# Expert stage of a hybrid decoder layer: from blocks of 64 rows on two column halves to steps of two 32-row sub-blocks on four column quarters

## The reference, cut to what matters

```
x1 = x + mix(rms_norm(x)) @ w_out            # attention, convolution and SSM heads
h  = rms_norm(x1)
group  = argmax(h @ group_w + group_b)        # 1 of 4 groups
expert = top 2 of the 8 experts of that group
y[t]   = sum over its 2 experts e: gate * ((silu(h@w_gate[e]) * (h@w_up[e])) @ w_down[e])
out    = rms_norm(x1 + y)
```

```
31 46 51 266 10 71 8 71 28 41 58 11 47 24 36 213 18 108 47 82 38 60 42 179 16 29 99 81 8 67 73 89
```

## Time and profile before

| what | value |
|---|---|
| median of 3 runs | 1182.27 us (1181.92 to 1182.78) |
| the profiled execution, its own time | 1182.57 us |
| its span | 1180.8 us |
| expert stage: first up/gate matmul to the end of the span | 565.6 to 1180.8 us |
| TensorE busy, share of the span | 94% |
| VectorE, ScalarE, GpSimd busy | 50%, 30%, 35% |

### The profile page before, as it was taken

One profiled execution on the slowest core, in us unless ns is written; L12 is line 12 of the kernel. 1 busy time (PEld: TensorE's weight loads), 2 busy tenths in 40 slices (PEclk: granted clock), 3 DMA queues, 4 the chain that ended last, 5 costly groups with the idle time before them and its releaser, 6 DMA issues.

```text
span 1180.8 us, 16952 instructions
## 1 busy us (share of the span) xinstructions
PE 1115.6 (94%) x5082; PEld 545.8 (46%) x5083; DVE 588.6 (50%) x1347; ACT 356.5 (30%) x719; POOL 410.9 (35%) x359
## 2 busy tenths in 40 slices
PE   5999999999999999997799999977999999999993
PEld 5898444445456666656333333322333333333331
DVE  3560009954556666546255554533454545555452
ACT  3222100025655555422132332312223323232231
POOL 0110099950000001010244545443345454444542
PEclk9999999999999999998899999989999999999998
DMA  8126212021231111159593799999969999999811
GB/s 265 25 37 126 53 22 52 8 71 39 96 157 62 58 43 54 55 226 369 191 403 80 286 391 392 413 407 415 413 248 406 407 417 413 402 416 402 349 29 33
DMA packets 91596, 257.71 MB, mean 218 GB/s; under 512 B 38867, under 2 KB 56026, under 8 KB 66942
## 3 DMA queue, kind: packets, MB, share of 16 engines
q1 hardware_dynamic: 66580, 234.78, 51.8%
q0 software_dynamic: 19232, 21.06, 6.5%
q10 hardware_dynamic: 5706, 0.92, 0.4%
HBM read 253.51 MB, written 35.13 MB: 244 GB/s over the span
## 4 chain that ended last, share of the span: by engine, by line
PE 83%; DMA 9%; ACT 2%; DVE 2%; issue 1%; SPq 1%; POOL 0%; ACTq 0%; DVEq 0%; POOLq 0%
PE psum L1386 25%; PE psum L1081 14%; PE psum L1405 12%; PE psum L1279 9%; DMA W<-in_w_down 5%; PE psum L1078 4%; PE psum L1224 3%; PE psum L1244 3%; DMA W<-in_w_gate 3%; PE psum L1076 3%; PE psum L1372 2%; PE psum L1235 2%; PE psum L1393 2%; PE psum L1308 1%; DMA W<-in_x 1%
## 5 line engine op out<-in xcount | busy, mean ns | idle before, releaser
L1386 PE MATMUL psum<-W,band 128*64 x400 | 187.7, 614 | 15.3 <-DVE W L1935 15.3
L1387 PE MATMUL psum<-W,band 128*64 128x512 f32 x400 | 187.7, 614 | 0.0
L1386 PE MATMUL psum<-W,RD 128*64 (+1 forms) x400 | 182.9, 601 | 2.5 <-DVE W L1935 1.5
L1405 PE MATMUL psum<-W,RD 128*64 (+1 forms) x400 | 180.0, 593 | 4.2 <-ACT RD L1010 2.6
L1387 PE MATMUL psum<-W,RD 128*64 128x512 f32 x400 | 182.9, 601 | 0.0
L1406 PE MATMUL psum<-RD 128*64 128x512 f32 x400 | 180.0, 593 | 0.0
L735 POOL DMA_INDIRECT x_rows<-RD,tabf x48 | 78.4, 1633 | 276.9 <-ACT RD L1018 266.0
L1081 PE MATMUL psum<-W 128*128 128x512 f32 x384 | 166.9, 594 | 0.4 <-ACT W L824 0.4
L1279 PE MATMUL psum<-W,RD 128*128 128x512 f32 x256 | 118.2, 594 | 1.6 <-ACT RD L900 1.1
L1081 PEld LDWEIGHTS psum<-W 128*128 128x128 f32 x384 | 72.5, 191 | 88.0 <-issue 87.1
L1386 PEld LDWEIGHTS psum<-W,band 128*64 128x64 f32 x400 | 54.0, 141 | 123.8 <-issue 120.8
(11 more groups left out here) (330 smaller groups left out, 1762.0 us busy)
## 6 DMA issues: line engine op xcount, KB each, us to landing
W<-in_w_up SPq DMA_DIRECT2D x32, 2048.0 KB, 13.2
W<-in_w_gate SPq DMA_DIRECT2D x32, 2048.0 KB, 19.0
W<-in_w_down SPq DMA_DIRECT2D x32, 2048.0 KB, 21.7
W<-in_x SPq DMA_DIRECT2D x16, 512.0 KB, 4.7
W<-in_w_in SPq DMA_DIRECT2D x5, 1024.0 KB, 11.6
W<-in_w_in SPq DMA_DIRECT2D x16, 256.0 KB, 4.4
x_rows<-W SPq DMA_DIRECT2D x8, 512.0 KB, 2.9
h_rows<-RD SPq DMA_DIRECT2D x8, 512.0 KB, 3.6
```

The lines of the kernel that those rows point to most:

```text
L1386: pe.matmul(bank(2)[0:HALF].rearrange("p (g n) -> p g n", g=2), x, near, start=k == 0, stop=k == KD - 1)
L1387: ins = pe.matmul(bank(2)[HALF:P], x, upgate1[:, k].rearrange("p g n -> p (g n)"), start=k == 0, stop=k == KD - 1)
L1405: pe.matmul(out[0:HALF], a, W[:, bass.ds(base + (2 * KD * FF + D * k), 512)], start=k == 0, stop=k == FK - 1)
```

## The change

Each expert now gets ceil(rows / 32) sub-blocks, at least one, 81 in all. A step takes two consecutive sub-blocks, A and B, each with its own expert, which may be the same: 41 steps. Each product over k is four matmuls on the four column quarters (32 rows held each): A near from the slot in place, A far from `farA`, B near and B far from `bothB`. ScalarE copies `farA` (512 numbers per partition and k), VectorE copies `bothB` (1024). Both are rings of four k steps, so a copy waits until the quarter products that used its buffer last are done (`used`), and the products of each k wait for both copies (`copied`). The square and sum of the finished rows moves from VectorE to ScalarE (`row_sum`). On GpSimd the rows come in earlier in the step, behind a wait for a scatter (`added`). All steps are written out, 32 of them always run, up to 16 more in nested conditions. `MAXPAIR` is 48. Lines that only rename or resize are left out below.

```diff
+def up_lap(b, part): return part if b == 0 else 3 * b - 1 + part
+def down_lap(b): return 3 * b + 4
...
+        def used(lap, j):        # the semaphore and value that tell that lap's use of buffer j is over
...
 pool.block_io(b):
-                if b >= 2:
-                    pool.wait_ge(ex_ye, b - 1)
-                    if b >= 3:
-                        pool.wait_ge(scat_out[(b - 1) % 2], 16 * ((b - 1) // 2))
-                    (scatter-add of block b-2)
+                if b >= 3:
+                    added(b - 3)
+                if b >= 1:
+                    x_in_rows(b - 1)
+                if b >= 2:
+                    pool.wait_ge(ex_ye, b - 1)
+                    (scatter-add of pair b-2)
                 gather(b + AHEAD); x_out_rows(b - 3); root(b - 2)
-                x_in_rows(b)
...
 act:
+            def step(b, before):
+                base, loads = tables(b)
+                silu_gate(b - 1)
+                weights_in(wug_in, loads, 32)
+                for j in range(4): far_up(base, up_lap(b, 0), j, j)
+                y_evac(b - 2)
+                for j in range(4): far_up(base, up_lap(b, 1), j, 4 + j)
+                actT_evac(b - 1)
+                row_sum(b - 2)
+                weights_in(wd_in, before[1], 16)
+                for k in range(FK): far_down(before[0], down_lap(b - 1), k)
...
 pe, for each k of up_gate (and alike for down):
-                    pe.matmul(bank(2)[0:HALF], x, near, ...)
-                    ins = pe.matmul(bank(2)[HALF:P], x, upgate1[:, k], ...)
+                    copied(lap, j)
+                    pe.matmul(out[0:SUB], xA, near, ...)
+                    pe.matmul(out[SUB:2 * SUB], xA, farA[j], ...)
+                    pe.matmul(out[2 * SUB:3 * SUB], xB, bothB[j][:, 0:512], ...)
+                    ins = pe.matmul(out[3 * SUB:P], xB, bothB[j][:, 512:1024], ...)
+                    ins.then_inc(ex_u if part == 1 and j == 3 else ex_k, 1)
+            def step(b, before):
+                up_gate(base, b, 0); aT(b - 1); xT(b + 1); up_gate(base, b, 1)
+                down(before, b - 1, down_lap(b - 1))
...
 dve:
+            def both_up(base, lap, j, k):
+                free(lap, j)                                  # wait for used(lap - 1, j)
+                dve.tensor_copy(bothB[j] ..., up and gate of k, all 2 x 512 columns).then_inc(ex_cB, 1)
+            def step(b, before):
+                base, loads = tables(b)
+                weights_in(wug_in, loads, 32)
+                both_up(0), both_up(1)
+                act_mul(b - 1)
+                both_up(2), both_up(3), both_up(4), both_up(5)
+                rows_add(b - 2)
+                both_up(6), both_up(7)
+                xT_evac(b + 1)                                # two instructions of 256 numbers
+                weights_in(wd_in, before[1], 16)
+                both_down(0), both_down(1)
+                rows_scale(b - 3)
+                both_down(2), both_down(3)
+                mean_square(b - 2)                            # four on 32 partitions each, one on 128
```

## The result

| | before | after |
|---|---|---|
| median of the comparison's runs | 1182.53 us (1181.92 to 1184.46, 4 runs) | 1204.93 us (1202.64 to 1207.33, 4 runs) |
| ratio, 95% interval | 1 | 1.0187 (1.016 to 1.0214) |
| the profiled execution, its span | 1182.57, 1180.8 us | 1206.59, 1204.5 us |
| TensorE, VectorE, ScalarE, GpSimd busy | 94, 50, 30, 35% | 86, 61, 47, 32% |
| mean granted clock of the span | 0.983 | 0.961 |

The change makes the kernel 1.9% slower, where 0.3% faster was forecast: 26 us off, inside the stated range. The step count (41) and the bounding engine are as forecast; the step is longer.

A forecast was written before the change was run, and what follows sets the result against it. VectorE was to bound the kernel at 13.3 us a step (TensorE 11.37). Expert 14's gate at 807.05 + 8.6 + 2.5 + 25 steps (332.5) + 0.6 + 2, then 24 to the end: span 1177.3, time 1179 us, range 1158 to 1222.

The forecast's parts named there:

- waits for the ring: VectorE's copies waiting for TensorE to free buffers: none expected, each free in time, slack 0.2 us in a 13.3 us step.
- GpSimd's hold: Rival: five GpSimd instructions each hold a VectorE copy 0.25 us; step 14.5, 1216 us; chance 0.21, shared with other waits.
- GpSimd gives way: GpSimd issues meeting VectorE copies: the issue stretches (2.29 us, median 1.05), copies keep their time; hidden under 13.3 us.
- the centre: The central forecast: VectorE's step 13.3 us, time 1179 us; chance 0.53 for a step of 13.0 to 13.7.
- The copies' sum: VectorE's step: 2.95 us to the first copy, twelve copies at 0.60 (7.2), plus smaller operations, 13.3 us.
- The clock: Rival: TensorE idles about 2 us every step, its clock falls each time, adding 2.5: step 15.8, 1256 us; chance 0.06.
- Late loads: Steps 10 to 16 wait some 40 us for weights; expert 14's gate lets VectorE copy at 807.05, no later waits.
- TensorE's overlap: Groups of four products run fully abreast, 0.853 us a group, step 11.37; rival of incomplete overlap, up to 1466 us, chance 0.06.
- ScalarE: ScalarE's step: twelve copies 6.5 us, other work about 2, reads and waits at most 2.95; 11.4, hidden under 13.3.

The follow-up runs named there:

- the new order: Changed kernel with VectorE's row scaling ahead of the first down copy and mean square ahead of the last: 1188.76 us; also without scatters and later gathers: 1163.93 us.

## Why the prediction was wrong

**The step that failed** is the account of what holds VectorE. It has two terms at nothing, waits for the ring and GpSimd's hold, and each alone makes the step 13.7 us: the first by the run without scatters and gathers, the second worked out from the trace of the changed kernel. The first is the account of waits: "With the first copy at 0, TensorE starts at 0.7 ... the first down copy at 6.5 needs the buffer used at 6.1. The slack is thin, 0.2 us, so 13.3 leans upward." Measured from the first copy: TensorE starts at 0.94 (911.62), not 0.7; its second group of part 1 starts at 6.31 (916.99), so the first buffer is used by then and the second by 7.17; VectorE starts the second down copy at 7.53, 0.36 behind that. This hand-over was not in the working. I had checked the first down copy alone, and its slack is 6.5 - 6.1 = 0.4, not 0.2; the second would start at 7.1 and needs the buffer used at 6.95, so its slack is 0.15. With the late start and the hand-over put in, 6.1 + 0.85 + 0.24 + 0.36 = 7.55, the same arithmetic gives +0.45 us. Without scatters and gathers this wait is there in full, 0.23 and 0.19 us, and the second down copy starts 0.5 us later than VectorE's own work would have it.

The second is "GpSimd gives way". In the changed kernel two copies of each undisturbed step are held, for 0.26 and 0.21 us, and that takes VectorE's own sum from 13.24 to 13.70, where the ring stands at 13.74. The extra 0.44 us cost 11.0 us in the 25 steps and 2.6 of the 4.6 before them. The text named the spot and the direction, had GpSimd's hold among its rivals, and then took the centre as if neither would come. That the time still lies inside the stated range is owed to the width of the range.

**The copies' sum was right.** Table reads and waits 2.9 (2.95 predicted), copies 0.60 apart, the others as taken; 2.9 + 9.4 + 1.45 less the 0.44 is 13.3. In the new order without GpSimd's two DMAs the step is 12.86: 0.5 of the last copy lies beside the reads, and 0.1 is the wait for TensorE.

**GpSimd** was cited as a rival at 14.5. Two of its five instructions in a step hold a copy; the other three lie beside the table reads and the mean square and hold none. So the term is 0.47 us and not 1.2. By the Trainium skill (SBUF — State Buffer, section Who interferes with whom) the shared port is an exclusive lock; the half that the earlier trace rows left unshown is in this trace now, copies of 0.95 and 0.90 beside issues and none above 0.70 without them. By the same section of the Trainium skill the one that comes second is blocked for the whole instruction of the other. This trace shows less: copies run on beside the scatter's issue of 2.20 us (912.26), and one of them is 0.26 us longer. In what order a held copy and an issue took the port no run shows.

**The clock** was a rival that could only come in every step or in none. It came in four of the last 25, after idle times of 2.35 to 2.83 us, while most of 2.2 to 2.4, and also 2.52, 2.68 and 3.01, kept 1.00: 7.3 us. The earlier trace rows showed one gap of 2.34 that kept the clock; one such row was no licence to price gaps just above it at nothing.

**Late loads** were right in kind: step 16 could copy at 811.6 (807 forecast), 3.2 us of it because the chain of loads began at 660.34 instead of 657.11. The loss is 37 us, not 40: from the first copy of step 9 (678.69) to that of step 16 pass 132.9 us, seven undisturbed steps take 96.2. The first copies waited 30 of it; the rest lies inside the steps, where TensorE ran at the low clock after waits, which the forecast counted only in step 16. **TensorE's overlap** is complete, where the Trainium skill (TensorE: Matmul & The Clock Gate, section Measured speedup vs the span model) has 3.07 for four products on row groups: here four long products over all 128 partitions take 0.43 us a pass, the time of a pair. **ScalarE** at 11.4 was nearly right: the step is 11.67 with its reads at the head once VectorE is out of the way, and 11.35 with them moved.

## What to carry to other kernels

Where two engines hand a ring of buffers to each other, write the loop down for every buffer, the last one of a batch first, with the hand-over in it; an engine's own sum is only one of two bounds. Where both give nearly the same step, taking away the cause of one shows nothing, so compare each with the measured step before calling it free. Register reads at the head of a step are serial time, yet free behind queued instructions: here 2.5 us of each step, worth 35 us in all. A gap on TensorE near the length at which the clock has fallen before can cost more than itself.

## What the runs showed of the hardware that was not expected

- Four register reads of 0.62 us each vanish when they stand behind queued copies: the gap falls from 2.9 to 0.4 us and the copies around them move by less than 0.1 us. VectorE's sequencer runs ahead of the engine. The text on the profile before says of such reads that an in-order engine does nothing else meanwhile; that holds only where nothing is queued ahead of them.
- When a copy waits for a group of products, it starts 0.36 us after the first pass of the next group has started (917.85 to 918.20). From the end of a copy to the first pass that waits for it there are 0.24 us (911.38 to 911.62).
- Scatters and gathers slow the loads. Without them GpSimd's queue falls from 6.3 to 2.3% of the 16 DMA engines' time, and the first copy of step 16 comes 14.5 us earlier, of which the chain of loads began 1.4 earlier. In the new order the chain begins at 656.1 in both kernels and the copy comes at 793.24 instead of 807.50.
- One more read of 0.6 us in the step brought the low clock into every second step; what decides between two gaps of the same length (2.80 us before 720.91 with a fall, 2.80 before 914.63 without, in that kernel) stays open.
